# Two kinds of product of a chunked recurrence taken together, on one core

## The reference, cut to what matters

```python
def wkv_scan(state0, r, w, k, v, kk, a, reverse):
    tm = lambda t: jnp.swapaxes(t, 0, 1)
    xs = (tm(r), tm(w), tm(k), tm(v), tm(-kk), tm(kk * a))
    def step(S, inp):
        r_t, w_t, k_t, v_t, nkk_t, b_t = inp
        sa = jnp.einsum('bhvk,bhk->bhv', S, nkk_t)
        S = S * w_t[:, :, None, :] + sa[..., None] * b_t[:, :, None, :] + v_t[..., None] * k_t[:, :, None, :]
        return S, jnp.einsum('bhvk,bhk->bhv', S, r_t)
    S_final, ys = lax.scan(step, state0, xs, reverse=reverse)
    return S_final, jnp.swapaxes(ys, 0, 1)
```

## Time and profile before

| | us |
|---|---|
| median of 3 executions | 4008.01 (3998.9 to 4016.06) |
| the profiled execution | 4019.99 |
| its span | 4018.2 |
| TensorE busy in the span | 3767.6 (94%) |
| VectorE busy | 2113.0 (53%) |
| ScalarE busy | 1586.7 (39%) |
| mean granted TensorE clock | 0.975 of full speed |

### The profile page before, as it was taken

How to read it: one execution, slowest core, us unless ns; L and a number is a source line. 1 busy time by engine, 2 the same in 40 slices (tenths; PEclk the granted TensorE clock), 3 DMA queues, 4 the chain that set the end, 5 groups by cost and what they waited for, 6 DMA issues and landing times.

```text
span 4018.2 us, 79245 instructions
## 1 busy us (share of the span) xinstructions
PE 3767.6 (94%) x34148; PEld 3299.5 (82%) x34148; DVE 2113.0 (53%) x2674; ACT 1586.7 (39%) x1993; POOL 1388.8 (35%) x632
## 2 busy tenths in 40 slices
PE   6878999899897899999998999998999999999998
PEld 5766888788886788888887888897788888888887
DVE  5698867666655687344445444435333443333433
ACT  3333226522113444444444444434344444444443
POOL 2332223000002355444443345444343434434342
PEclk9999999999998999999999999999999999999999
DMA  7887863000003577555554555454555555555553
GB/s 289 298 286 242 298 225 100 25 4 4 4 11 105 170 254 247 183 189 189 184 183 137 177 173 177 156 171 152 174 188 173 168 174 175 177 174 172 170 168 129
DMA packets 183546, 670.49 MB, mean 167 GB/s; under 512 B 20480, under 2 KB 20480, under 8 KB 182432
## 3 DMA queue, kind: packets, MB, share of 16 engines
q1 hardware_dynamic: 176832, 644.17, 48.5%
q10 hardware_dynamic: 5088, 17.07, 1.2%
q0 software_dynamic: 1280, 4.20, 0.3%
HBM read 656.97 MB, written 8.39 MB: 166 GB/s over the span
## 4 chain that ended last, share of the span: by engine, by line
PE 78%; DVE 11%; ACT 3%; issue 3%; DMA 2%; PEld 1%; POOL 1%; ACTq 0%; PEldq 0%; DVEq 0%; POOLq 0%; SPq 0%
PE ps L1032 62%; DVE whl L1996 2%; DVE raw L2094 2%; PE ps L1276 2%; PE ps L1252 2%; PE ps L1266 1%; ACT whl L1502 1%; PE ps L1188 1%; PEld ps L1032 1%; DVE tm L1999 1%; DVE ch L2090 1%; DVE halves L1999 1%; ACT work L1502 1%; PE ps L1490 1%; PE ps L1474 1%
## 5 line engine op out<-in xcount | busy, mean ns | idle before, releaser
L1032 PE MATMUL ps<-halves,whl 128*128 128x256 f32 (+1 forms) x14752 | 2600.5, 337 | 113.6 <-DVE whl L1996 24.5
L1032 PEld LDWEIGHTS ps<-halves,whl 128*128 128x128 f32 x14752 | 2249.3, 191 | 434.9 <-issue 109.3
L2613 POOL TENSOR_TENSOR whl<-raw,whl 128x1024 fp32r<-128x1024 f32 x508 | 1256.7, 2474 | 1796.7 <-ACT whl L1502 1796.6
L1502 ACT ACTIVATE whl<-raw 128x1024 fp32r<-128x1024 f32 x1016 | 1057.9, 1053 | 990.1 <-PE ps L1032 712.7
L1996 DVE TENSOR_TENSOR whl<-raw,whl 128x1024 fp32r<-128x1024 f32 x508 | 782.6, 1541 | 1084.8 <-ACT whl L1502 1084.7
L1032 PE MATMUL ps<-whl,halves 128*128 128x256 f32 x2752 | 491.1, 337 | 25.2 <-DVE whl L1996 15.7
L1032 PEld LDWEIGHTS ps<-whl,halves 128*128 128x128 f32 x2752 | 421.2, 190 | 85.3 <-issue 22.5
L2094 DVE SCALAR_TENSOR_TENSOR raw<-raw,mix 128x1024 f32<-128x1024 f32 x160 | 273.1, 1726 | 5.7 <-DMA raw<-in_adaT 4.6
L1502 ACT ACTIVATE work<-ps 128x512 f32<-128x512 f32 (+1 forms) x200 | 116.2, 584 | 304.2 <-PE ps L1032 252.7
L2613 POOL TENSOR_TENSOR halves<-mix,halves 128x1024 fp32r<-128x1024 f32 (+1 forms) x16 | 27.7, 1738 | 552.8 <-ACT halves L1502 552.8
L1996 DVE TENSOR_TENSOR work<-work,ps 128x512 f32<-128x512 f32 x157 | 107.4, 684 | 102.4 <-ACT work L1502 101.4
(11 more groups left out here) (260 smaller groups left out, 2509.2 us busy)
## 6 DMA issues: line engine op xcount, KB each, us to landing
raw<-in_ffn SPq DMA_DIRECT2D x264, 512.0 KB, 4.3
raw<-in_w_kv SPq DMA_DIRECT2D x192, 512.0 KB, 3.5
raw<-in_adaT SPq DMA_DIRECT2D x160, 512.0 KB, 5.1
raw<-in_w_in_b SPq DMA_DIRECT2D x160, 512.0 KB, 3.4
raw<-in_w_in_a SPq DMA_DIRECT2D x128, 512.0 KB, 3.8
raw<-in_mem SPq DMA_DIRECT2D x64, 512.0 KB, 4.8
raw<-in_w_out_a SPq DMA_DIRECT2D x48, 512.0 KB, 3.7
raw<-in_w_out_b SPq DMA_DIRECT2D x48, 512.0 KB, 4.0
```

The costliest lines, as they stand in the source:

```text
L1032: p = self.e.matmul(o, x, y, start=bi not in begun, stop=final and kc == 3 and m == len(pairs) - 1, skip_group_check=True)
L1502: return self.e.activation(out, in_, func, **kw)
L2613: return self.e.tensor_tensor(out, a, b, op)
```

## The change

`pre_k` and `pre_ak` have the same stationary operand (a head of kh), and so have `pre_b` and `pre_bt` (a head of bh). The change takes each two as one product with 128 moving columns: the 64 of ar and the 64 of the unit matrix. The results of a head lie side by side in PSUM, so one pair of banks holds four of the eight heads of each partition half; the work is done in two halves.

- Steps of a preparation are now v, b (half 0), b (half 1), x, xt, k (half 0), k (half 1), then btr and akr from n = 4 on: as many steps, and as many pairs of banks, as before.
- Each new block is 16 products of 64 by 64 by 128, on the same four quarters of the array. The moving operand has two strides: 64 columns of ar, and 64 of a unit matrix that now lies behind the 1024 elements of ar in a tile `ari0` or `ari1`; the distance between the two depends on the head.
- TensorE's `pre_b` waits for bh and for ar before its first product; `pre_k` waits for kh.
- VectorE masks BT and AKA by `masked`: two instructions of 128 by 256 for each half, four for what was one of 128 by 1024. `arr` is made after BT of the second half.
- ScalarE copies btok and ktok in two halves each, and after VectorE has read the same banks.
- `rwkv_begin` on VectorE waits for the constants and copies the unit matrix behind both ar tiles. Tiles t, X0, ar, PP, hk and gate1 move to other addresses.

```diff
-        self.pre_k(n, self.take())
-        yield
-        self.pre_b(n, self.take())
-        yield
-        self.pre_bt(n, self.take())
-        yield
+        for half in range(2):
+            self.pre_b(n, half, self.take())
+            yield
         self.pre_x(n, self.take())
         yield
         self.pre_xt(n)
         yield
-        self.pre_ak(n, self.take())
-        yield
+        for half in range(2):
+            self.pre_k(n, half, self.take())
+            yield
...
+    def four_heads(self, k):
+
+        return self.ps[:, k:k + 2, :].rearrange("p x (c a n) -> p x c a n", c=4, a=2)
...
+    def with_unit(self, n, r, d, c):
+
+        i = 64 * (8 * d + c)
+        step = 1024 - i
+        return self.A(f"ari{n % 2}")[r, i:i + 2 * step].rearrange("p (a n) -> p a n", a=2)[:, :, 0:64]
+
+    def pairwise(self, n, half, k, lhs, name, done):
+
+        self.two_banks(k, "pre_s", done)
+        o = self.four_heads(k)
+        for c in range(4 * half, 4 * half + 4):
+            for s, r in enumerate(HALF):
+                for d, h in enumerate(HALF):
+                    m = self.e.matmul(o[h, s, c % 4, :, :], lhs[r, d, c, :], self.with_unit(n, r, d, c), start=True, stop=True)
+        m.then_inc(self.sig("pre_mm", (n, (name, half))), 1)
+
+    def pre_b(self, n, half, k):
+        self.wait_ge("ld_rwkv", 3)
+        self.wait_ge("pre_v", (n, "bh"))
+        self.wait_ge("pre_v", (n, "ar1"))
+        self.pairwise(n, half, k, self.joint["u"], "b", (n, ("btok", half)))
+
+    def pre_k(self, n, half, k):
         self.wait_ge("pre_v", (n, "kh"))
+        self.pairwise(n, half, k, self.joint["t"], "k", (n, ("kt", half)))
...
+    def pre_b(self, n, half, k):
+        self.wait_ge("pre_v", (n, ("BT", half)))
+        self.act(self.sets[n % 2]["btok"][:, :, 4 * half:4 * half + 4, :], self.four_heads(k)[:, :, :, 1, :], ACT.Copy).then_inc(
+            self.sig("pre_s", (n, ("btok", half))), 1)
...
+        self.wait_ge("ld_rwkv", 3)
+        for p in range(2):
+            self.e.tensor_copy(self.A(f"ari{p}")[:, 1024:1088], self.rwc[:, 576:640]).then_inc(self.own(), 1)
...
+    def masked(self, n, half, k, name):
+
+        for s in range(2):
+            m = self.tt(self.sets[n % 2][name][:, s, 4 * half:4 * half + 4, :], self.four_heads(k)[:, s, :, 0, :], self.mask(448, 4), MUL)
+            m.then_inc(self.sig("pre_v", (n, (name, half) if s else (name, half, 0))), 1)
+
+    def pre_b(self, n, half, k):
+        self.wait_ge("pre_mm", (n, ("b", half)))
+        self.masked(n, half, k, "BT")
+        if n >= 4 and half:
             tx = self.tokens(n, 4)
             for c in range(4):
                 self.wait_ge("ev_v", (("w_r", c, 0), 0))
             for d in range(2):
                 self.tt(self.sets[n % 2]["arr"][:, d], self.PP[:, d, :, 1:65], self.rT[:, :, tx[d]], MUL).then_inc(self.sig("pre_v", (n, f"arr{d}")), 1)
```

More of the change, by code:

```diff
@@ L314, in names @@
             q = {n: A(n + str(p)).rearrange("p (x c n) -> p x c n", x=2, c=8) for n in
-                 ("ar", "AKA", "btok", "ktok", "vtok", "Xt", "X", "BT")}
+                 ("AKA", "btok", "ktok", "vtok", "Xt", "X", "BT")}
+            q["ar"] = A(f"ari{p}")[:, 0:1024].rearrange("p (x c n) -> p x c n", x=2, c=8)
             for n, v in (("arr", A("kk")), ("AKAr", self.kT), ("BTr", self.vT)):
@@ L750 @@
     out_rest = no_steps
-    pre_lw = pre_ab = pre_decay = pre_v = pre_kd = pre_kh = pre_k = pre_b = pre_bt = pre_x = pre_xt = pre_ak = pre_btr = pre_akr = nothing
+    pre_lw = pre_ab = pre_decay = pre_v = pre_kd = pre_kh = pre_k = pre_b = pre_x = pre_xt = pre_btr = pre_akr = nothing
     adv_av = adv_r = adv_u = adv_z = adv_yz = adv_y = inv_t1 = inv_x = inv_xt = nothing
@@ L1281, in adv_av @@
         self.r_out = o = self.two_banks(k, "adv_s", (n, "R"))
-        self.wait_ge("pre_v", (n, "AKA"))
+        self.wait_ge("pre_v", (n, ("AKA", 1)))
         self.wait_ge("pre_s", (n, "vt"))
@@ L1323, in adv_z @@
         o = self.two_banks(k, "adv_v", (n, "z1" if n else "z"))
-        self.wait_ge("pre_s", (n, "kt"))
+        self.wait_ge("pre_s", (n, ("kt", 1)))
         self.by_token(o, q["ktok"], q["vtok"], True, False)
-        self.wait_ge("pre_s", (n, "btok"))
+        self.wait_ge("pre_s", (n, ("btok", 1)))
         self.wait_ge("adv_s", (n, "U"))
@@ L1791, in pre_v, with pre_k @@
         self.act(self.A(f"vtok{n % 2}"), self.pair(k), ACT.Copy).then_inc(self.sig("pre_s", (n, "vt")), 1)
[L1793 to L1799, removed]
+    def pre_b(self, n, half, k):
+        self.wait_ge("pre_v", (n, ("BT", half)))
+        self.act(self.sets[n % 2]["btok"][:, :, 4 * half:4 * half + 4, :], self.four_heads(k)[:, :, :, 1, :], ACT.Copy).then_inc(
+            self.sig("pre_s", (n, ("btok", half))), 1)
+    def pre_k(self, n, half, k):
+        self.wait_ge("pre_v", (n, ("AKA", half)))
+        self.act(self.sets[n % 2]["ktok"][:, :, 4 * half:4 * half + 4, :], self.four_heads(k)[:, :, :, 1, :], ACT.Copy).then_inc(
+            self.sig("pre_s", (n, ("kt", half))), 1)
     def adv_r(self, n, k):
@@ L2326, in pre_k @@
                 self.tt(self.sets[n % 2]["arr"][:, d], self.PP[:, d, :, 1:65], self.rT[:, :, tx[d]], MUL).then_inc(self.sig("pre_v", (n, f"arr{d}")), 1)
-    def pre_bt(self, n, k):
-        self.wait_ge("pre_mm", (n, "bt"))
-        self.tt(fc16(self.A(f"BT{n % 2}")), self.bank16(k), self.mask(448, 16), MUL).then_inc(self.sig("pre_v", (n, "BT")), 1)
+    def pre_k(self, n, half, k):
+        self.wait_ge("pre_mm", (n, ("k", half)))
+        self.masked(n, half, k, "AKA")
     def pre_x(self, n, k):
@@ L2790, in memory @@
         at(n, hbl + 4 * i * K, [1024])
+    at("ari0", phc + 2816, [2048])
+    at("ari1", hal + 8 * K, [2048])
     at("aup", mx + 16 * K, [1024])
```

38 lines of the change are left out of this document (8 added, 30 removed).

## The result

The changed kernel took 4023.92 us (median of 7 runs, 4014.81 to 4034.59). The kernel before took 4008.01 us (median of 7 runs on the same chip, 3998.90 to 4016.94). The ratio is 1.0033, with a 95% interval from 1.0016 to 1.0049. So it is slower by a third of a per cent, where faster was forecast, and outside the predicted range. The profiled execution took 4021.55 us, its span 4019.7.

The account below looks back on a forecast made before the run. Instruction supply was taken to nearly bound the recurrence (417 of 445 us), with VectorE bounding parts. Per-preparation gains, less 1.2 us in chunk 0 and 0.3 for copies, summed to 15.4 us: 4008.0 to 3992.6, say 3993; range 3974 to 4012.

Parts of the forecast that it names:

- Supply: TensorE in the recurrence: 256 instructions fewer per preparation, one packet, 3.79 us; at most 30.3 us for eight.
- the slower rival: TensorE's gaps are not instruction supply and stay, so the wait for ar costs 19 us: 4027; chance 0.1.
- The time of a new block: Joined block of 32 records on four quarters of TensorE's array: taken as 0.9 us, 0.86 at best.
- the 1.33 of the rival: Weight loads do not hide on TensorE: a new block takes 1.33 us, 5 us won, 4003; chance 0.15.
- The wait for ar: First product with bh waits for ar, made 2.9 us after kh; x ends 6.55 us after ar in chunk 3.
- Its chain from X to the last Xt: VectorE's masks and T behind x in chunk 4: 8.75 us, busy without a break.
- forecast gain: Each preparation's win from less supply, after the ar wait and added VectorE work; whole sum 15.4 us.
- -1.2 + 1.3 = 0.1: Chunk 0 loses 1.0 us at X and 0.2 for AKA; chunk 1, taken like chunk 3, wins 1.3 us.

Follow-up runs that it names:

- second profile: Kernels before, after and with the wait filled, each unchanged and profiled once more; recurrence 467.6, 486.7 and 466.0 us.
- filled wait: Changed kernel with twelve unread products of 512 columns ahead of pre_b's wait for ar in chunks 0 to 5; 4007.22 us, ratio 1.0003.
- block before: Changed kernel with an empty step ahead of pre_b, so a block of the inversion runs where TensorE waited; 4003.60 us, ratio 0.9995.
- the wait alone: Kernel before with only pre_k's first product made to wait for ar, not kh; 4029.41 us, ratio 1.0055.
- two small moves of order: Changed kernel with an empty step ahead of pre_b and kh made behind the first mask of BT; 3991.42 us, ratio 0.9948.

## Why the prediction was wrong, step by step

**Supply: right in kind, its size not settled.** Eight packets fewer, and the "issue" waits of three rows go with the count: 27.8 us with 113 packets in the recurrence (23.3 in the second profile), 19.3 with 109, 10.4 with 105. So the point named for the slower rival (the gaps stay) did not come. What a packet is worth in time is not shown: half a packet taken away alone gave 2.4 and 1.65 us against one profile of the kernel before, 0.8 and 0.5 against the other. The Trainium skill, "Runtime: NRT & Kernel Launch", "Instruction fetch mechanics", calls the fetch mostly hidden; in this recurrence these waits do not agree with that.

**The time of a new block: right at the upper clock.** 0.88 us for 30 records in the chain, and 0.90 from the start of one block to the next in the filled wait (916.51 to 917.41), for a forecast of 0.9; the 1.33 of the rival did not come. At 1.2 GHz it is 1.98.

**The wait for ar: its length right, its price wrong.** "The old pre_k needed only kh; bh, a T and ar are made after it, 1.1 + 0.6 + 1.2 = 2.9 us": it measured 2.95 us of idle time in preparation 3, and up to 3.3. In preparation 6 it was 1.6, where under 0.5 was forecast. The step that failed is the next: "From 910.3 the array then needs b 0.9, a double block of the inversion 1.9, b 0.9, a double block 1.9, x 0.95: 6.55 us". It took 12.3 (927.36 to 937.93 + 1.76 = 939.69), with the clock at 0.50 for all of it. That the stage would fall from 0.98 to 0.92 of the clock was nowhere in the sum.

**VectorE: right behind X.** Its chain from X to the last Xt was forecast at 8.75 us and without a break. In preparation 3 it runs from 939.73 to 948.46, 8.73 us, with no idle time in it.

**What the sum was without it.** Intervals from one adv_av to the next, each with one preparation in it, from the records of the first profiles:

| preparation | before | forecast gain | filled wait | after | low clock behind pre_b, after |
|---|---|---|---|---|---|
| 2 | 49.5 | 2.5 | 47.6 | 51.5 | 10.2 |
| 3 | 50.3 | 1.3 | 50.4 | 54.7 | 13.7 |
| 4 | 53.2 | 2.1 | 51.9 | 57.4 | 13.7 |
| 5 | 53.7 | 2.1 | 51.7 | 54.1 | 3.4 |
| 6 | 61.0 | 3.8 | 56.8 | 56.5 | 3.4 |
| 7 | 59.4 | 3.8 | 54.5 | 56.2 | 0 |

With the wait kept and only its idle time filled, the six preparations gain 14.2 us, where the terms add to 15.6. In the kernel after, 6 and 7 gain 4.5 and 3.2, near the forecast, and 2 to 5 lose 11.0 in place of gaining 8.0. By the second profiles the six preparations gain 3.1 with the wait filled, and in the kernel after 6 and 7 gain 2.7 and 1.8 and 2 to 5 lose 18.3. So the loss in 2 to 5 is seen both times, and the good agreement of the gains is in part luck. Preparations 0 and 1, up to the first adv_av, took 73.9 us for 65.7 (8.2 more), where -1.2 + 1.3 = 0.1 was forecast as gain.

**A page that bears on the missing term.** The Trainium skill, "TensorE: Matmul & The Clock Gate", section "HAM oscillation — how this bites in real kernels", describes a kernel in which a wait that recurs drops the clock each time, and prices it at the throttled time by (1 - 1.2/2.4). By it, the estimate for the change is (85.3 - 30.7) / 2 = 27 us. The trace agrees in kind. In size the profiles give 23 us for 61.4 us at the lower clock in the kernel after, and 3.7 for 41.0 in the kernel before, where the supply of instructions seems to be the limit anyway.

**Slower, but not by the rival named.** The slower rival gave 4027 and the measured time is 4024, yet its mechanism (gaps that stay) is refuted. That the number came near is luck.

**What stays open.** With the filled wait the runs show no gain over the kernel before (1.0003), though the recurrence of the first profile is 13 us shorter; by the second profiles it is 1.6. Whether 13 or 2 is nearer is not settled. Nor do the whole times of single profiles help: the part of the program outside the recurrence took from 3531 to 3556 us in them. So of the 28 us between the forecast gain of 15.4 and the measured loss of 13, the timed runs give 12 to the clock behind the wait, the recurrence 21 to 23; the rest has no cause that the runs show. Why the clock fell at 913.7 and 1012.7 us with the block before is not settled either. In every profile but those of the change and of the wait alone 24 to 51 us at the lower clock are left, most of it in preparations 0 and 1 and at the end of the recurrence.

## What to carry to other kernels

A wait that a change puts on TensorE can be priced twice: by its length, and by the clock of what runs behind it. So look at the granted clock in the stretches behind the waits that the profile already has, and at how long these waits are. If a wait cannot be shortened below them, put other products ahead of it, or make the operand earlier; here two small moves of order turned a loss of 0.3% into a gain of 0.5%. Where the supply of instructions is the limit, count instructions and not columns. And before an effect of a few us is read from one profile, profile the same kernel twice: here one stretch of 23 us took 21.4 the next time.

## What the runs showed of the hardware that was not expected

- In a stage where TensorE is 91% busy (403.63 of 445 us), idle times of 3.0 us were mostly followed by 10 to 14 us at half clock, and once by 3.4. Idle times of 1.8 us were followed by none in four preparations of one kernel and by 10.2 us in one of another; of three of 2.15 us in one kernel one was followed by 10.2 us, one by 3.4, one by none. Products with no use, 2.75 us of them ahead of the wait, prevented it.
- 32 records of 64 by 64 by 128 on four quarters took 0.90 us at 2.4 GHz, near the 0.86 that the prediction works out for the columns alone: the weight loads of products that share rows and follow each other add next to nothing there. At 1.2 GHz they took 1.98.
- A 32-bit product of 64 by 64 by 64 is four instructions, and a packet of the instruction queue held 256 instructions. The waits for "issue" in preparation 3 of the kernel before ended 3.79 us apart, and the array took 1.9 us for 256 instructions of such products on four quarters, 3.7 on two. With such small products the supply of instructions can be as much of a limit as the array.
